# Every second low part of the gate tiles on GpSimd, one-hots with a PSUM operand, and picks on eight places for the low ranks

## The chip, the cores and the metric

One of the cores of a Trainium2 chip runs the whole kernel. The metric is the device time of one execution in microseconds, lower is better; it is given as the median of several executions.

## The reference, cut to what matters

Two layers work on 512 tokens of width 1024. Each layer has a token mixer (not touched here) and then a feed-forward part that picks experts by product keys. Only that part matters for the change:

```
q = (ht @ w_q).reshape(t, 8, 2, 128)
sc = einsum('thid,hikd->thik', q, keys)            # 16 score rows of 128 keys per token
top_s, top_i = lax.top_k(sc, 16)
cand = top_s[:, :, 0, :, None] + top_s[:, :, 1, None, :]
best_s, best_pos = lax.top_k(cand.reshape(t, 8, 256), 16)
i1 = take_along_axis(top_i[:, :, 0], best_pos // 16)
i2 = take_along_axis(top_i[:, :, 1], best_pos % 16)
gates = softmax(best_s)                            # experts = i1 * 128 + i2
act = einsum('thkd,td->thk', u_tab[experts], hb)   # u_tab, v_tab: 16384 rows of 1024
out = einsum('thk,thkd->td', gates * gelu(act), v_tab[experts])
```

## The kernel before, in words

**The stream of tiles.** All weights of a layer, and both expert tables as dense matrices, come as one stream of 298 tiles of 128 x 1024 float32: 18 for the input projection, 8 for the output, 16 for the queries, 128 tiles of `u_tab` (from index `U0`) and 128 of `v_tab` (from `EV0`). SyncE loads a tile into one of three buffers `w_raw`. ScalarE copies it rounded to fp32r (`hi`, line 755, `w_hi`), and somebody subtracts (`lo`, `w_lo = w_raw - w_hi`): VectorE on line 1593 or GpSimd on line 696. TensorE multiplies in three passes, high by high, high by low and low by high, 24 matmuls for a tile (`project`, line 1037). There are two buffers of `w_hi` and of `w_lo`, so both parts of tile n+2 can only be made once TensorE has finished tile n (semaphore `s_tile`), and tile n+2 waits for both (`s_wh`, `s_wl`). A buffer of `w_raw` is given back to SyncE when both are made.

**Two kinds of tokens.** Of the 512 tokens, 352 (`TD`) go through the dense product with all 16384 experts. The other 160 have their own expert rows gathered from HBM by indirect DMAs: 160 gathers of `u` rows and 160 of `v` rows per layer, 128 rows of 4 KB each. The gathers go through a ring of five buffers (`RING`). GpSimd issues them in order (line 708); gather k+5 waits until VectorE has used gather k (`s_gd`). VectorE uses a `u` gather with one multiply-and-sum on line 2087.

**The stages of the 128 u tiles of a layer.** Call n the index of a u tile.

- Routing, n up to about 41: beside the tiles, VectorE finds the candidates, the best 16 pairs and the indices of each of four blocks of 128 tokens. `picked(tt, a)` (lines 2175 to 2185) turns the place of each pair (128 places, `HK`: 8 heads times 16 ranks) into a key by three operations on a 128 x 2048 tile `pick`: compare, multiply, sum. It runs twice per block. In this stage GpSimd makes the low parts of tiles 2 to 38 (`POOL_LO0` to `POOL_LO1`) and issues 16 early gathers. When VectorE has finished with the routing, it waits for GpSimd's last low part and goes on with the gate stage.
- Gates, n from 42 to 101 (`GATE0`, `GATE1`): tokens are handled four at a time, a "quad". There are 88 quads; `quads_of(n)` gives one to even n and two to odd n. For each quad VectorE makes the one-hot matrices of both key indices (`one_hots`, line 2109, 128 x 1024 elements: `iota` compared with `idxT`, both in SBUF), ScalarE scales one half by the gate (line 960, four operations a quad), TensorE multiplies them (four matmuls, lines 1521 and 1535), and ScalarE copies the result out of PSUM (line 991). Four buffers `oneh`, two PSUM banks. Part of the gate matrices stays in SBUF, and part is stored to HBM in bursts of four.
- The rest, n from 102, then 128 tiles of `v_tab` (line 1553), beside them the `v` gathers on VectorE (line 2099).

**Orders written out by hand.** There is no scheduler; each engine runs its own program in order. In step n VectorE does `U_GATHERS[n]` gathers (1 or 2, seven in four tiles of the gate stage), the one-hots of quads of n+1, and `lo` of tile n+2. ScalarE does the scaling of quads of n, `hi` of n+2, the gelu of tile n (line 967), and the copies of the quads of n. GpSimd has a list `POOL_GATE_LO` of gate tiles whose low parts it would make; it is empty, so in the gate stage GpSimd only issues gathers. The code for it stands in GpSimd's loop over n from `GATHER0` to `GATE1`:

```
used += U_GATHERS[n]
if n + 2 in POOL_GATE_LO:
    pool.wait_ge(s_wl, l * STREAM + U0 + n + 2)
    lo(l, U0 + n + 2)
while k < used + RING:
    gather(l, k)
    k += 1
```

Its counterpart on VectorE skips `lo` for a tile of that list, and before the `lo` of the tile behind one waits for it on `s_wl`.

Of the kernel before, what the change touches and what calls it, by code (L numbers as in the profile page):

```python
# [9 lines left out]
ALU = mybir.AluOpType  # L10
ACT = mybir.ActivationFunctionType
AX = mybir.AxisListType

P = 128
# [44 lines left out]
PH = 8  # L59
TOPK = 16  # L60
HK = PH * TOPK
# [34 lines left out]
GATE0 = 42  # L96
GATE1 = 102
GATE_LOOP = 8
OH_SLOTS = 4
# [6 lines left out]
def quads_of(n):  # L106

    if not GATE0 <= n < GATE1:
        return []
    i = n - GATE0  # L110
    first = i // 2 * 3 + i % 2
    return [q for q in ([first] if i % 2 == 0 else [first, first + 1]) if q < QUADS]
# [28 lines left out]
    U_GATHERS[_n] = 2 if _n % 5 in (1, 3) else 1  # L141
U_GATHERS[GATE1 + 4] = U_GATHERS[GATE1 + 14] = 1
assert sum(U_GATHERS) + EARLY == UG and U_GATHERS[N_KEYS - 1] == 0, sum(U_GATHERS)
POOL_GATE_LO = []
V_GATHERS = [0] + [2 if _b % 4 == 3 or _b in (33, 65, 97) else 1 for _b in range(1, N_KEYS - 1)] + [0]
assert sum(V_GATHERS) == UG, sum(V_GATHERS)

# [33 lines left out]
class Steps:  # L181
# [16 lines left out]
    def link(self, ins):  # L198

        ins.then_inc(self.sem, 1)  # L200
        self.n += 1
        self.eng.wait_ge(self.sem, self.n)


def build(nc, xT, cT, final_g, adaw, wst, params, keysT, u_0, u_1, v_0, v_1, g_dram, a_dram, outT):
    u_rows, v_rows = (u_0, u_1), (v_0, v_1)
    ctx = ExitStack()
    with ctx:
        def sb(name, shape, dt=F32, where=ctx):
            return where.enter_context(nc.sbuf_tensor(name, shape, dt))  # L210
# [10 lines left out]
        iota = sb("iota", [P, P])  # L221
# [51 lines left out]
        def pcol(name, n=None):  # L273
            a, w = PCOL[name]
            return par[:, a:a + w]
# [110 lines left out]
        route = sb("route", [P, 3, HK], where=r2)  # L386
# [4 lines left out]
        oneh = [sb(f"oneh{s}", [P, 2, QUAD, P], where=r3) for s in range(2)]  # L391
# [261 lines left out]
        def _(pool):  # L653
# [59 lines left out]
            for l in range(LAYERS):  # L713
# [16 lines left out]
                for n in range(GATHER0, GATE1):  # L730
# [3 lines that stand above are left out]
# [845 lines left out]
        def _(dve):  # L1579
            steps = Steps(dve, s_dve, s_dset)  # L1580
            link = steps.link
            v = nc.vector
# [43 lines left out]
            for j, p0, w in ((0, 0, 2), (0, 64, 4), (1, 0, 8), (1, 64, 16)):  # L1626
                ins = v.tensor_scalar(inv_count[p0:p0 + 64, j, :], inv_count[p0:p0 + 64, j, :], float(w), None, ALU.min)
# [18 lines left out]
            for l in range(LAYERS):  # L1646
# [22 lines left out]
                for k in range(KT):  # L1669
                    ins = v.tensor_scalar(h32[:, k, :], h32[:, k, :], mod[:, 0, k:k + 1], None, ALU.add)  # L1670
                ins.then_inc(s_h32, 1)

                q = lambda n: tiny[:, n, :]
# [143 lines left out]
                def averaged(p0, j, src):  # L1817

                    r = slice(p0, p0 + 64)
                    v.tensor_tensor(pooled[r, j, 0:PAD], src[r, j, PAD:2 * PAD], inv_count[r, j, :], ALU.mult)  # L1820
                    return v.tensor_scalar(pooled[r, j, PAD:], src[r, j, 2 * PAD:], inv_count[r, j, PAD - 1:PAD], None, ALU.mult)

                for n in range(N_IN):
# [21 lines left out]
                    if n == 13:  # L1845
                        dve.wait_ge(s_pm, l + 1)
                        for j in range(2):
                            ins = v.tensor_scalar(mixed[:, 4 + j, :], bank[2 + 4 * j][:, :], pcol("pool_scale")[:, j:j + 1], None, ALU.mult)
# [25 lines left out]
                    if n == 11:  # L1874
                        link(v.tensor_tensor(pool_a[:, 1, 15:], pool_c[:, 1, 15:], pool_c[:, 1, 7:PJW - 8], ALU.add))
                        for p0, j, src in ((0, 1, pool_c), (64, 1, pool_a)):
                            ins = averaged(p0, j, src)
# [225 lines left out]
                def one_hots(q):  # L2103

                    n = l * QUADS + q
                    if n >= OH_SLOTS:
                        dve.wait_ge(s_gm, n - OH_SLOTS + 1)
                    full = [P, 2, QUAD, P]
                    v.tensor_tensor(oneh[q % OH_SLOTS][:, :, :, :], iota[:, :].unsqueeze(1).unsqueeze(1).broadcast_to(full),  # L2109
                                    idxT[:, 0:2, q * QUAD:(q + 1) * QUAD].unsqueeze(3).broadcast_to(full),  # L2110
                                    ALU.is_equal).then_inc(s_oh, 1)

                first_at = bank[5][:, 0:HK]
# [5 lines left out]
                full = [P, PH, TOPK, TOPK]  # L2119
                each = lambda f: [f(h) for h in range(PH)][-1]  # L2120
                pk = pick[:, :, :]
                pk4 = pk.rearrange("p (h k) j -> p h k j", h=PH)
# [52 lines left out]
                def picked(tt, a):  # L2175

                    at, of, op, rows = ((first_at, pair_start[:, :], ALU.is_ge, step_at),
                                        (col_at, iota[:, 0:TOPK], ALU.is_equal, row_at))[a]
                    link(v.tensor_tensor(pk, at.unsqueeze(2).broadcast_to([P, HK, TOPK]),
                                         of.unsqueeze(1).broadcast_to([P, HK, TOPK]), op))  # L2180
                    link(v.tensor_tensor(pk4, pk4, rows.unsqueeze(2).broadcast_to(full), ALU.mult))
                    if a == 0 and tt >= 2:

                        dve.wait_ge(s_rtt, l * (NT - 1) + tt - 1)
                    link(v.reduce_sum(route[:, a, :], pk, AX.X))

                def gated(tt):

# [31 lines left out]
                for tt in range(NT):  # L2220
                    first_rows(tt)
                    candidates(tt)
                    best_pairs()
                    shifted()
                    decoded()
                    early = EARLY_GATHERS[tt]
                    if tt == 1:
                        dve.wait_ge(s_htr, l + 1)
                    for a in range(2):
                        for _ in range(early // 3):  # L2230
                            gather_u(gathered)
                            gathered += 1
                        picked(tt, a)
                    for _ in range(early - 2 * (early // 3)):
                        gather_u(gathered)
                        gathered += 1
                    gated(tt)
                    if tt == 2:
                        extra_gathers()

                def coefs(b):

                    g, j = b // GROUP, b % GROUP
                    s = g % 2
                    if j == 0:

                        dve.wait_ge(s_gin[s], (l * (GROUPS // 2) + g // 2 + 1) * 16)
                        dve.wait_ge(s_ain[s], (l * (GROUPS // 2) + g // 2 + 1) * 16)
                    act = act_in[s][:, j // 2, j % 2, :]
                    v.tensor_tensor(coef[:, b % 2, 0:GSPILL].rearrange("p (c t) -> p c t", c=GSTORED),  # L2250
                                    act[:, 0:GSPILL].rearrange("p (c t) -> p c t", c=GSTORED),
                                    gates[s][:, :, j, :], ALU.mult)
                    v.tensor_tensor(coef[:, b % 2, GSPILL:TD].rearrange("p (c t) -> p c t", c=GKEPT),  # L2253
                                    act[:, GSPILL:TD].rearrange("p (c t) -> p c t", c=GKEPT),
                                    stages[:, :, b, :], ALU.mult).then_inc(s_cp, 1)
# [6 lines left out]

                k = EARLY
                assert gathered == EARLY
                dve.wait_ge(s_htv, 2 * l + 2)
                dve.wait_ge(s_wl, l * STREAM + POOL_LO1)
                for n in range(GATHER0, N_KEYS):
                    for _ in range(U_GATHERS[n]):
                        gather_u(k)
                        k += 1  # L2270
                    if n == GATE0 - 1:
                        dve.wait_ge(s_idx, l * (NT - 1) + NT - 1)
                    for q in quads_of(n + 1):
                        one_hots(q)
                    if n == N_KEYS - 2:
                        dve.wait_ge(s_gv, (l + 1) * QUADS + 2)
                    if n >= N_KEYS - 2:
                        coefs(n - (N_KEYS - 2))
                    if n + 2 not in POOL_GATE_LO:
                        if n + 1 in POOL_GATE_LO:  # L2280
                            dve.wait_ge(s_wl, l * STREAM + U0 + n + 2)
                        lo(l, U0 + n + 2)
                    if n >= N_KEYS - 2:
                        coef_low(n - (N_KEYS - 2))
                assert k == UG

                k = 0
# [106 lines left out]
```

## Time and profile before

| | us |
|---|---|
| median of 3 runs | 2919.84 |
| lowest and highest | 2913.98, 2921.28 |
| the profiled execution, its own time | 2915.25 |
| its span | 2913.5 |
| TensorE busy in the span | 2854.0 (98%) |
| VectorE busy | 2495.6 (86%) |
| ScalarE busy | 1447.4 (50%) |
| GpSimd busy | 998.9 (34%) |

The span is cut into stretches by what the engines work on. The u tiles of the first layer start near 400 us, its gate stage runs from about 571 to 876 us, and its v tiles start at 980 us. For the second layer the gate stage runs from about 1987 to 2293 us. A matmul's recorded duration overlaps the next one's, so TensorE's progress is read from the starts of its pieces in the chain of waits, not from durations of single matmuls.

### The profile page before, as it was taken

Reading aid. Unit: us, or ns where it says so; the run is one execution under the profiler, and the core shown is the slowest. Engines: PE = TensorE matmul, PEld = TensorE weight load, DVE = VectorE, ACT = ScalarE, POOL = GpSimd, SP = SyncE. Lnnn points to the kernel's source line nnn. Section 1 sums busy time; section 2 is a strip of 40 time slices with the busy share of each in tenths; the row PEclk is TensorE's granted clock in tenths of the full one; section 3 lists DMA queues with packets and bytes.
Section 4 is the critical chain, followed back from the end, with each engine's and each line's share of the span. In section 5 each row is a group of like instructions: output and inputs, shape, how many; then the busy total and the mean of one; then the engine's idle time right before and its main releaser. Section 6 shows DMA issues by size and latency. Waiting matters only on the chain.

```text
span 2913.5 us, 48879 instructions
## 1 busy us (share of the span) xinstructions
PE 2854.0 (98%) x17734; PEld 2666.3 (92%) x17734; DVE 2495.6 (86%) x4773; ACT 1447.4 (50%) x2309; POOL 998.9 (34%) x773
## 2 busy tenths in 40 slices
PE   6999999999999999999999999999999999999998
PEld 4777789999999999999978778999999999999998
DVE  5667789799996899999986779988999879999998
ACT  3345234488883433333353532447888634333333
POOL 1000027644443443444400000675444333443442
PEclk9999999999999999999999999999999999999999
DMA  7435647899999999999931122679999999999996
GB/s 277 169 114 187 255 145 239 304 363 380 393 330 383 360 381 381 382 386 385 379 117 66 66 69 84 200 245 348 394 375 372 345 379 364 387 380 377 378 386 250
DMA packets 261579, 857.75 MB, mean 294 GB/s; under 512 B 25664, under 2 KB 58688, under 8 KB 254784
## 3 DMA queue, kind: packets, MB, share of 16 engines
q1 hardware_dynamic: 158336, 445.11, 41.8%
q0 software_dynamic: 98496, 381.73, 34.9%
q10 hardware_dynamic: 4608, 29.36, 2.4%
q8 instruction: 51, 0.84, 0.1%
q14 instruction: 88, 0.72, 0.1%
HBM read 778.50 MB, written 77.59 MB: 294 GB/s over the span
## 4 chain that ended last, share of the span: by engine, by line
PE 83%; DMA 7%; DVE 5%; ACT 3%; issue 2%; SPq 0%; POOL 0%; DVEq 0%; ACTq 0%
PE banks L1037 39%; PE banks L1553 29%; PE banks L1521 4%; DMA w_raw<-wst 4%; PE banks L1358 2%; DMA ring<-u,gidx 2%; PE banks L1053 2%; DVE w_lo L1593 2%; PE banks L1102 1%; ACT w_hi L755 1%; PE banks L1441 1%; DMA pj<-adaw 1%; DVE ring L2087 1%; DVE oneh L2109 1%; PE banks L1199 0%
## 5 line engine op out<-in xcount | busy, mean ns | idle before, releaser
L755 ACT ACTIVATE w_hi<-w_raw 128x1024 fp32r<-128x1024 f32 x596 | 630.3, 1058 | 747.8 <-PE banks L1037 575.0
L1037 PE MATMUL banks<-hH,w_hi 128*128 128x352 f32 (+1 forms) x2528 | 866.4, 343 | 4.8 <-issue 1.7
L1593 DVE TENSOR_TENSOR w_lo<-w_raw,w_hi 128x1024 fp32r<-128x1024 f32 x522 | 638.4, 1223 | 269.8 <-ACT w_hi L755 247.8
L1037 PE MATMUL banks<-hH,w_lo 128*128 128x352 f32 (+1 forms) x2528 | 845.4, 334 | 0.0
L1037 PE MATMUL banks<-hL,w_hi 128*128 128x352 f32 (+1 forms) x2528 | 845.0, 334 | 0.0
L708 POOL DMA_INDIRECT ring<-v,gidx x320 | 396.1, 1238 | 593.0 <-DVE vacc L2099 534.6
L708 POOL DMA_INDIRECT ring<-u,gidx x320 | 399.1, 1247 | 464.7 <-DVE gact L2087 438.9
L1037 PEld LDWEIGHTS banks<-hH,w_hi 128*128 128x128 f32 x2528 | 474.8, 188 | 53.5 <-issue 24.4
L1553 PE MATMUL banks<-c_lo_late,w_hi 128*128 128x352 f32 x1536 | 494.0, 322 | 0.0
L1037 PEld LDWEIGHTS banks<-hH,w_lo 128*128 128x128 f32 x2528 | 474.3, 188 | 19.5
L1037 PEld LDWEIGHTS banks<-hL,w_hi 128*128 128x128 f32 x2528 | 475.1, 188 | 17.4 <-issue 0.5
L2099 DVE SCALAR_TENSOR_TENSOR vacc<-ring,gcoef,vacc 128x1024 f32<-128x1024 f32 x316 | 404.2, 1279 | 7.4 <-DVE vacc L2099 0.5
L2087 DVE CUSTOM_DVE_ANT_0 ring<-ring,banks 128x1024 f32<-128x1024 f32 x256 | 304.1, 1214 | 50.4 <-DMA ring<-u,gidx 26.3
L696 POOL TENSOR_TENSOR w_lo<-w_raw,w_hi 128x1024 fp32r<-128x1024 f32 x74 | 177.8, 2402 | 472.1 <-ACT w_hi L755 471.2
L1553 PE MATMUL banks<-c_hi_late,w_hi 128*128 128x352 f32 x1024 | 334.5, 327 | 1.7 <-DVE w_lo L1593 1.5
L1553 PE MATMUL banks<-c_hi_first,w_hi 128*128 128x352 f32 x1024 | 332.7, 325 | 0.0
L1553 PE MATMUL banks<-c_hi_first,w_lo 128*128 128x352 f32 x1024 | 330.8, 323 | 0.0
L1553 PE MATMUL banks<-c_hi_late,w_lo 128*128 128x352 f32 x1024 | 329.9, 322 | 0.0
L1553 PEld LDWEIGHTS banks<-c_lo_late,w_hi 128*128 128x128 f32 x1536 | 289.2, 188 | 0.0
L960 ACT ACTIVATE oneh<-oneh,idxT 128x128 f32<-128x128 f32 x704 | 215.3, 395 | 8.6 <-DVE oneh L2109 6.9
L2109 DVE TENSOR_TENSOR oneh<-iota,idxT 128x1024 f32<-128x1024 f32 x176 | 209.7, 1218 | 0.0
L1012 ACT ACTIVATE c_hi_late<-coef 128x352 fp32r<-128x352 f32 x128 | 63.8, 498 | 289.3 <-DVE coef L2253 289.3
(345 smaller groups left out, 3986.4 us busy)
## 6 DMA issues: line engine op xcount, KB each, us to landing
w_raw<-wst SPq DMA_DIRECT2D x596, 512.0 KB
activations<-act_out SPq DMA_DIRECT2D x128, 352.0 KB
act_in<-activations SPq DMA_DIRECT2D x64, 704.0 KB
gate_matrices<-stages ACTq DMA_DIRECT2D x32, 896.0 KB
gates<-gate_matrices SPq DMA_DIRECT2D x64, 448.0 KB
ada_buf<-adaw POOLq DMA_DIRECT2D x24, 1024.0 KB, 6.5
nrm<-adaw POOLq DMA_DIRECT2D x8, 1024.0 KB, 5.1
pj<-adaw POOLq DMA_DIRECT2D x7, 1024.0 KB, 7.2
```

What stands on the lines that cost most here:

```text
L696: pool.tensor_tensor(w_lo[g % 2][:, :, :].rearrange("p a b -> p (a b)"), w_raw[:, g % RAWS, :], w_hi[g % 2][:, :, :].rearrange("p a b -> p ...
L708: pool.indirect_dma_start(out=ring[:, n % RING, :], out_offset=None, in_=rows[:, :], in_offset=bass.IndirectOffsetOnAxis(ap=gidx[:, k % UG ...
L755: nc.scalar.activation(w_hi[g % 2][:, :, :].rearrange("p a b -> p (a b)"), w_raw[:, g % RAWS, :], ACT.Copy).then_inc(s_wh, 1)
L960: ins = nc.scalar.activation(oh, oh, ACT.Copy, scale=idxT[:, 2, q * QUAD + t:q * QUAD + t + 1])
L1012: nc.scalar.activation(c_hi[(b + 2) % GROUP], coef[:, b % 2, :], ACT.Copy).then_inc(s_chi, 1)
L1037: last = mm(bank[s][:, 0:t.stop - t.start], a[s][:, k, :], b[:, k, t], start=(k == 0 and a is w_hi and b is hH), stop=(k == KT - 1 and a i ...
L1521: last = mm(bank[2 + u % 2][:, t * P:(t + 1) * P], oneh[u % OH_SLOTS][:, 0, t, :], oneh[u % OH_SLOTS][:, 1, t, :], start=True, stop=True)
L1553: last = mm(bank[k][:, TG:T], w[j % 2][:, k, :], c[j], start=(first and w is w_hi and c is c_hi), stop=(final and w is w_lo))
L1593: v.tensor_tensor(w_lo[g % 2][:, :, :].rearrange("p a b -> p (a b)"), w_raw[:, g % RAWS, :], w_hi[g % 2][:, :, :].rearrange("p a b -> p (a ...
L2087: v.tensor_tensor_reduce(ring[:, n % RING, :], ring[:, n % RING, :], rhs, 1.0, 0.0, ALU.mult, ALU.add, gact[:, k:k + 1]).then_inc(s_gd, 1)
L2099: ins = v.scalar_tensor_tensor(acc[:, :], ring[:, n % RING, :], gcoef[:, k:k + 1], acc[:, :], ALU.mult, ALU.add)
L2109: v.tensor_tensor(oneh[q % OH_SLOTS][:, :, :, :], iota[:, :].unsqueeze(1).unsqueeze(1).broadcast_to(full), idxT[:, 0:2, q * QUAD:(q + 1) * ...
```

## The change

- `POOL_GATE_LO` is filled with the 29 gate tiles n that stand behind a tile of two quads: 44, 46, ... 100. GpSimd makes their low parts, VectorE no longer does.
- The one-hots read the column numbers from PSUM (`first_at`, in bank 5) instead of SBUF (`iota`). One copy a layer puts them there, behind the routing.
- `picked` works on two boxes. The low ranks (0 to 7 of each head) are compared with 8 places only, the others with 16: 8 x 8 x 8 = 512 and 8 x 8 x 16 = 1024 elements instead of 2048. So each of the three operations is now two.

```diff
-POOL_GATE_LO = []
+POOL_GATE_LO = [n for n in range(GATE0, GATE1) if len(quads_of(n - 1)) == 2]
...
-                    v.tensor_tensor(oneh[q % OH_SLOTS][:, :, :, :], iota[:, :].unsqueeze(1).unsqueeze(1).broadcast_to(full),
+                    v.tensor_tensor(oneh[q % OH_SLOTS][:, :, :, :], first_at.unsqueeze(1).unsqueeze(1).broadcast_to(full),
                                     idxT[:, 0:2, q * QUAD:(q + 1) * QUAD].unsqueeze(3).broadcast_to(full),
                                     ALU.is_equal).then_inc(s_oh, 1)
...
-                    link(v.tensor_tensor(pk, at.unsqueeze(2).broadcast_to([P, HK, TOPK]),
-                                         of.unsqueeze(1).broadcast_to([P, HK, TOPK]), op))
-                    link(v.tensor_tensor(pk4, pk4, rows.unsqueeze(2).broadcast_to(full), ALU.mult))
+                    boxes = [(slice(0, 8), 8), (slice(8, TOPK), TOPK)]
+                    by_rank = lambda t: t.rearrange("p (h k) -> p h k", h=PH)
+                    for ranks, w in boxes:
+                        box = [P, PH, 8, w]
+                        ins = v.tensor_tensor(pk4[:, :, ranks, 0:w], by_rank(at)[:, :, ranks].unsqueeze(3).broadcast_to(box),
+                                              of[:, 0:w].unsqueeze(1).unsqueeze(1).broadcast_to(box), op)
+                    link(ins)
+                    for ranks, w in boxes:
+                        ins = v.tensor_tensor(pk4[:, :, ranks, 0:w], pk4[:, :, ranks, 0:w],
+                                              rows[:, :, 0:w].unsqueeze(2).broadcast_to([P, PH, 8, w]), ALU.mult)
+                    link(ins)
...
-                    link(v.reduce_sum(route[:, a, :], pk, AX.X))
+                    for ranks, w in boxes:
+                        ins = v.reduce_sum(by_rank(route[:, a, :])[:, :, ranks], pk4[:, :, ranks, 0:w], AX.X)
+                    link(ins)
...
+                link(v.tensor_copy(first_at, iota[:, :]))
                 dve.wait_ge(s_htv, 2 * l + 2)
                 dve.wait_ge(s_wl, l * STREAM + POOL_LO1)
```

## Rows read from the trace of the kernel before

**Rows 1.** The chain of waits, gate stages of both layers: start us, duration us, what.

```profile
579.59 1.78 PE banks L1521 x16
...
591.66 3.81 PE banks L1037 x24
595.47 0.89 PE banks L1521 x8
...
871.62 3.81 PE banks L1037 x24
...
2008.23 3.81 PE banks L1037 x24
...
2288.28 3.81 PE banks L1037 x24
```

**Rows 2.** Engine busy time by stretch, first layer: routing (two), gates (three).

```profile
core 0: us, PE busy (x) PEld busy (x) DVE busy (x) ACT busy (x) POOL busy (x), PEclk, DMA share, GB/s
400.00:490.00 90.00, 90.00 (x560) 86.93 (x559) 86.53 (x356) 37.10 (x51) 58.32 (x30) 1.00 0.63 205
490.00:572.00 82.00, 80.69 (x500) 78.24 (x500) 64.13 (x141) 36.28 (x52) 56.61 (x33) 1.00 0.80 270
572.00:660.00 88.00, 88.00 (x617) 88.00 (x616) 86.08 (x106) 77.27 (x161) 41.14 (x31) 1.00 0.97 371
660.00:750.00 90.00, 89.39 (x622) 88.83 (x622) 82.06 (x102) 79.47 (x165) 38.45 (x30) 1.00 1.00 388
750.00:880.00 130.00, 129.91 (x905) 129.48 (x904) 122.87 (x153) 111.26 (x234) 56.81 (x46) 1.00 0.95 349
```

**Rows 3.** VectorE's waits, both routing stages: total us, times, longest us.

```profile
DVE ring L2087 <- POOL w_lo L696: 11.5, 1, 11.5
DVE ring L2087 <- POOL w_lo L696: 12.0, 1, 12.0
```

**Rows 4.** Groups of VectorE instructions by line and shape: busy us, mean ns.

```profile
L1593 DVE TENSOR_TENSOR w_lo<-w_raw,w_hi 128x1024 fp32r<-128x1024 f32 x522 | 638.4, 1223 | 269.8 <-ACT w_hi L755 247.8 <-issue 20.2
L2109 DVE TENSOR_TENSOR oneh<-iota,idxT 128x1024 f32<-128x1024 f32 x176 | 209.7, 1218 | 0.0
L2181 DVE TENSOR_TENSOR pick<-pick,banks 128x2048 f32<-128x2048 f32 x16 | 36.6, 2287 | 0.6
L2185 DVE TENSOR_REDUCE route<-pick 128x128 f32<-128x2048 f32 x16 | 36.6, 2286 | 0.6
L1779 DVE TENSOR_TENSOR smat<-seg,cbm 128x512 f32<-128x512 f32 x16 | 10.3, 684 | 0.0
```

**Rows 5.** Single lines 696 (GpSimd) and 2212 (VectorE): duration ns min/median/max.

```profile
L696 POOL TENSOR_TENSOR w_lo<-w_raw,w_hi x74: 2372/2402/2428, 403.7 to 1967.6; 128x1024 fp32r<-128x1024 f32 x74
L2212 DVE COPY ggate<-pick x2: 1406/1836/2266, 507.9 to 1922.8; 128x32 f32<-128x32 f32 x2
```

**Rows 6.** Timeline of GpSimd in the gate stage: start us, duration us, instruction, idle before.

```profile
822.29 0.94 POOL L708 DMA_INDIRECT ring<-u,gidx  x1 [1.73 <-DVE gact L2087]
823.69 1.43 POOL L708 DMA_INDIRECT ring<-u,gidx  x1 [0.45 <-DVE gact L2087]
828.22 0.94 POOL L708 DMA_INDIRECT ring<-u,gidx  x1 [3.10 <-DVE gact L2087]
```

**Rows 7.** Timeline of VectorE, the same stretch.

```profile
820.80 1.21 DVE L2087 CUSTOM_DVE_ANT_0 ring<-ring,banks 128x1024 f32<-128x1024 f32 x1
...
823.09 2.35 DVE L2109 TENSOR_TENSOR oneh<-iota,idxT 128x1024 f32<-128x1024 f32 x2
825.36 1.22 DVE L1593 TENSOR_TENSOR w_lo<-w_raw,w_hi 128x1024 fp32r<-128x1024 f32 x1
826.50 1.21 DVE L2087 CUSTOM_DVE_ANT_0 ring<-ring,banks 128x1024 f32<-128x1024 f32 x1
```

**Rows 8.** Timeline of ScalarE, the same stretch.

```profile
824.09 1.06 ACT L755 ACTIVATE w_hi<-w_raw 128x1024 fp32r<-128x1024 f32 x1 [1.21 <-issue]
```

**Rows 9.** VectorE's waits for gathers in the first layer's gate stage.

```profile
DVE ring L2087 <- DMA ring<-u,gidx: 8.5, 6, 2.2
```

**Rows 10.** The chain of waits, around 741 us.

```profile
724.79 16.54 DMA ring<-u,gidx
...
742.58 2.28 DVE oneh L2109 x2
744.86 0.27 issue
745.13 1.13 PE banks L1521 x8
```

## The prediction

> **What bounds the kernel now.** I read the chain of waits first, because a change that takes work off VectorE and puts it on GpSimd only matters where one of them ends the chain. In the gate stage the chain is TensorE alone, and it runs like a clock [rows 1]: a u tile takes 3.81 us, one quad behind it 0.89, two quads 1.78. So two tiles with their three quads take 2 x 3.81 + 3 x 0.89 = 10.29 us. From tile 46 (591.66) to tile 100 (871.62) there are 27 such pairs: 277.8 us if TensorE never waits, and 279.96 were taken. In the second layer it is 2288.28 - 2008.23 = 280.05. So TensorE loses 2.1 and 2.2 us, 4.4 us in both gate stages together. That is all that relief of VectorE can bring there.
>
> The busy time by stretch agrees, and adds what the chain doesn't say [rows 2]: in the gate stage VectorE is busy 86.08 of 88 us, ScalarE 77.27, and the DMA engines 95 to 100%. Four resources are nearly full, TensorE is the fullest, and the others have to hit its beat. Where VectorE is late, it is so because a gather has not landed: six waits, 8.5 us in the first layer's gate stage [rows 9]. One of them stands in the chain [rows 10]: a gather issued at 724.79 landed 16.54 us later, the two one-hots came late, and their quads started late on TensorE. So the thing to watch is the ring of gathers, which hangs on GpSimd.
>
> In the routing stage VectorE, when done, waits 11.5 and 12.0 us for GpSimd's last low part [rows 3]. Its routing work is not late for anything.
>
> **The change, part by part.**
>
> *Picks.* A compare, multiply or sum over 2048 elements takes 2.29 us; 512 take 0.68, 1024 take 1.22 [rows 4]. Two boxes: 0.68 + 1.22 = 1.90, so 0.38 saved each. There are 3 x 2 x 4 x 2 = 48 of them: 18.4 us off VectorE, 9.2 a layer. The time goes into the wait for GpSimd at the end of routing, which grows from 11.5 to about 21 us [rows 3]. TensorE is busy 90.00 of 90 us beside the bulk of it [rows 2], so nothing comes nearer. I count 0; the end below is -1 us a layer if some early gather is used sooner, above 0.
>
> *The copy to PSUM.* Two copies of 128 x 128, under 0.68 us each by the 512-element row [rows 4], inside the same wait: 0.
>
> *One-hots from PSUM.* The form with two SBUF operands takes 1.218 us, multiplications with one PSUM operand lie on the same line (2.287 for twice the size) [rows 4]. So the duration stays: 0. What it may change is GpSimd: its gather issues take 0.94 us, but 1.43 when one begins beside a running one-hot (823.69 against 823.09) [rows 6, 7]. That half microsecond I take back for about half of the issues; it goes into the ring's account below. The Trainium skill, "SBUF — State Buffer", section "SBUF: two separate sides", has it that VectorE and GpSimd share one pair of ports under an exclusive lock, taken by VectorE operations with two SBUF inputs. By that rule the one-hots would no longer hold up GpSimd's subtraction at all, and the trace agrees as far as it goes: the stretched issue above, and a copy of 32 elements that took 1.4 and 2.3 us in the routing stage, where GpSimd subtracts [rows 5].
>
> *Low parts on GpSimd.* 29 tiles x 2 layers. VectorE gives up 58 x 1.223 = 70.9 us [rows 4], GpSimd takes on 58 x 2.402 = 139.3 us [rows 5]. Is the low part itself in time? `hi` starts at 824.09, when the even tile n has ended, and VectorE's `lo` follows at 825.36 [rows 7, 8]. On GpSimd it would end near 825.3 + 2.4 = 827.7. Tile n+2 needs it after a quad, a tile and two quads: 824.03 + 0.89 + 3.81 + 1.78 = 830.5. Slack 2.8 us: 0 for the low part itself.
>
> The price is behind it in GpSimd's queue. The gathers released in step n now stand behind `lo` of n+2. The slots that VectorE freed around 822 and 823 were given to new gathers at 822.29 and 823.69 [rows 6]; now the first goes out at 827.8 and the second 1.25 later: 5.4 us later each. Those of the odd step, freed near 827.6 and so far issued from 828.22 [rows 6], wait for these two: about 1 to 2 us later. With three to four gathers in a pair of tiles, about half of them of each kind, a slot loses 3 us on average. A slot comes round every 5/7 of four tiles, 20.58 x 5/7 = 14.7 us. So far issue to use leaves some 13 us for the gather; now 10, for the worst ones 8. Gathers under the bursts of gate stores take more than that: the one at 724.79 took 16.5 [rows 10].
>
> Against it stands VectorE's relief: 1.14 us a pair of tiles (a low part, starts lie 1.14 apart [rows 7]), so it arrives earlier at the next gather, and the wait of the `lo` behind GpSimd's is for `hi` anyway. Also fewer transfers lie in the DMA queues when issues come late, so each lands sooner after its issue. I put it so: the gate stage has three places a layer where a late gather reaches TensorE (they make up the 2.1 us). A slot 3.0 us later, less two pairs' relief of 1.1 each, leaves about 1 us more at each place: 3 x 2 x 1 = +6 us. This is an estimate from the rows above; the ends are -4.4 us (all of TensorE's waits go) and +18 us (each place passes on the 3.0 us in full).
>
> *Sum.* 2915.25 us (the profiled execution; 2913.5 of it span, 1.75 around it) + 0 + 0 + 0 + 6 = 2921.3 us. The median of the runs shown is 4.6 us above that execution, which gives 2925.8. The next median may lie on either base; I take 2924.
>
> **The rivals.**
>
> *A. VectorE's relief removes the late gathers.* If the ring's slots have enough room in spite of GpSimd, the one-hots come early and TensorE's 4.4 us go: 2919.84 - 4.4 = 2915.4. For it: VectorE is 98% busy in the first stretch of gates. Against: its waits there are for gathers, which it can't shorten [rows 9].
>
> *B. Nothing moves.* The picks' time goes into a wait, the relief into idle time, the ring holds: 2920. For it: 98% TensorE.
>
> *C. The ring becomes the bound, slower.* GpSimd's queue holds back the gathers of even steps by 5.4 us; under the bursts of gate stores a gather takes 12 to 16 us, a slot cycle then takes longer than 14.7 us, VectorE is late in several pairs in a row, its one-hots are late, and TensorE waits. It decides from the point at which issue to landing exceeds 10 us for more than three gathers in a row. Price: 3 us at each of six places, +18 us: 2938. For it: DMA share 1.00 at 388 GB/s in the middle stretch [rows 2], the row of 16.54 us. Against: gathers outside the bursts cause no wait at all.
>
> *D. The two engines stop each other.* If VectorE's operations wait out a GpSimd subtraction after all (with the gathers' multiply, say), each of the 58 puts up to 2.4 us on VectorE against 1.14 taken off: 58 x 1.26 = +73 us, 2993. Against it: in the routing stage GpSimd's subtractions took 2372 to 2428 ns [rows 5] beside a VectorE that was busy 86.53 of 90 us [rows 2]. The copy of 32 elements shows that such stops exist, but for a form that the gate stage doesn't have.
>
> **How the numbers follow.** Forecast (a small loss, +1 to +9 us): 0.42. B, with A's smaller part (-4 to +1): 0.24. A: 0.07. C: 0.23. D: 0.04. A measurement of this kernel can tell about 0.3% from no change, 8.8 us; the runs shown lie 7.3 us apart. Faster by more than that: 0.08, since the chain has only 4.4 us to give and the rest would be another base. Slower by more: most of C, D and the edge of the forecast, 0.32. Same: 0.60. Range: from 2911 (A on the lower runs) to 2939 (C).
>
> **What would show it.** In the changed profile: GpSimd has 132 subtractions instead of 74, near 2.40 us each; if they are longer, D. VectorE's busy time falls by about 89 us. Its wait at the end of routing grows to about 21 us; if it doesn't, the picks are mispriced. One-hots stay at 1.22 us. Gather issues in the gate stage are near 0.94 us each. From tile 46 to tile 100: 283 us rather than 280 by the forecast, 278 by A, 286 or more by C. VectorE's waits for gathers in a gate stage grow from 8.5 us to over 20; if they stay below 10, the account of the ring is wrong, and with it the forecast. Most wrong would be a gain of more than 10 us: then TensorE's beat in the gate or routing stage was not what the chain shows.

## The result and the profile after

The changed kernel takes 2944.26 us, median of 4 runs (2937.6 to 2949.99), against 2918.28 us for the kernel before beside it (4 runs). The ratio is 1.009, 95% interval 1.0074 to 1.0105: it is 26 us slower. The forecast was 2924 us, the range ended at 2939. The profiled execution's span went from 2913.5 to 2940.9 us, +27.4. Two executions, one of the kernel before and one of the version with both mends, took 4019 and 4714 us at a granted clock of 0.65 and 0.56 where all others have 0.99; no median or ratio below includes them.

The page's head shows what the change did, and that it did what it says: VectorE gave up 80.6 us of busy time, GpSimd took on 88.3.

```profile
span 2940.9 us, 48931 instructions
...
PE 2865.1 (97%) x17734; PEld 2673.7 (91%) x17734; DVE 2415.0 (82%) x4765; ACT 1448.8 (49%) x2309; POOL 1087.2 (37%) x831
...
L696 POOL TENSOR_TENSOR w_lo<-w_raw,w_hi 128x1024 fp32r<-128x1024 f32 x132 | 317.3, 2404 | 665.2 <-ACT w_hi L755 665.2
...
L2109 DVE TENSOR_TENSOR oneh<-banks,idxT 128x1024 f32<-128x1024 f32 x176 | 209.7, 1219 | 0.0
```

GpSimd's 132 subtractions take 2.404 us each, the one-hots 1.219 us: neither became longer than before. The time is between the operations. (A few small operations of the routing stage did become longer; they are named below.) This is the chain of waits of the changed kernel, first layer (start, duration, what); it answers to [rows 1].

```profile
575.63 3.81 PE banks L1037 x24
...
591.51 3.81 PE banks L1037 x24
...
884.48 3.81 PE banks L1037 x24
888.28 0.89 PE banks L1535 x8
889.17 7.61 PE banks L1037 x48
```

From tile 46 (591.51) to tile 100 (884.48) it is now 293.0 us, where it was 280.0, and in the second layer 293.7 against 280.1. From tile 43 to tile 101 the two stages grew from 300.5 and 300.8 to 313.5 and 314.6 us: 26.8 of the 27.4 us of span are here. TensorE's beat itself is the same, 3.81 and 0.89 us. It loses at three places a layer: at tiles 56 to 58 (5.3 and 5.8 us in the two layers), 75 and 76 (3.1 and 2.6) and 84 to 86 (5.9 and 5.6). Each lies just behind one of the layer's four bursts of gate stores; the second burst costs 0.7 and 1.8 us. The kernel before loses 1.1 and 1.3 us at tile 76, 0.7 and 0.2 at tile 86, and nothing at tiles 56 to 58. The first place in the chain of the changed kernel:

```profile
622.37 3.82 PE banks L1037 x24
...
626.27 1.07 ACT w_hi L755
...
627.50 2.41 POOL w_lo L696
629.91 0.14 issue
630.05 0.95 POOL ring L708
631.00 0.30 issue
631.30 15.13 DMA ring<-u,gidx
...
647.69 1.15 DVE oneh L2109
648.84 1.40 issue
650.24 1.33 PE banks L1521 x8
```

Read it as one sentence: tile 52 ends, ScalarE rounds tile 54, GpSimd subtracts, issues one gather, then the next, this one takes 15.13 us, VectorE uses it and makes a one-hot, and only then TensorE has its quad. GpSimd's timeline there (start, duration, instruction, idle before) shows three issues in a heap behind the subtraction:

```profile
627.50 2.41 POOL L696 TENSOR_TENSOR w_lo<-w_raw,w_hi 128x1024 fp32r<-128x1024 f32 x1 [2.35 <-ACT w_hi L755]
630.05 0.95 POOL L708 DMA_INDIRECT ring<-u,gidx  x1
631.30 0.94 POOL L708 DMA_INDIRECT ring<-u,gidx  x1 [0.30 <-issue]
632.55 1.65 POOL L708 DMA_INDIRECT ring<-u,gidx  x1 [0.31 <-issue]
637.79 2.42 POOL L696 TENSOR_TENSOR w_lo<-w_raw,w_hi 128x1024 fp32r<-128x1024 f32 x1 [3.59 <-ACT w_hi L755]
```

The same gather in the kernel before, where tile 52 starts at the same time (622.52 us), first its issue, then its use on VectorE:

```profile
630.22 0.94 POOL L708 DMA_INDIRECT ring<-u,gidx  x1 [3.91 <-DVE gact L2087]
...
640.25 1.22 DVE L2087 CUSTOM_DVE_ANT_0 ring<-ring,banks 128x1024 f32<-128x1024 f32 x1
```

It left only 1.1 us sooner, but had landed within 10.0 us. So in the changed kernel it left late, and it also took 5 us longer. The gather two before it fared the same. It no longer leaves ahead of the burst, whose first store goes out at 623.2 us: issued at 624.2 us it took 13.7 us, and 6.7 us in the run with the list empty (below), where it left at 621.7. The six gathers that stand in the chain at the six places all belong to odd steps. Each came second or fourth in such a heap, 3.7 or 4.6 us after its slot was free.

And VectorE's waits in the first layer's gate stage (total us, times, longest) answer to [rows 9], where there were 8.5 us in six waits, the longest 2.2:

```profile
DVE w_lo L1593 <- ACT w_hi L755: 32.7, 23, 2.8
DVE ring L2087 <- DMA ring<-u,gidx: 32.3, 18, 3.4
```

### The profile page after: what moved, and what is told of

Same layout as the page of the kernel before. It is cut to its first block, busy times and chain, and to the rows that moved or that the text cites. A ratio compares the mean times of both kernels' runs of the same rounds, so it can differ in the third digit from the quotient of the medians.

```text
span 2940.9 us, 48931 instructions
## 1 busy us (share of the span) xinstructions
PE 2865.1 (97%) x17734; PEld 2673.7 (91%) x17734; DVE 2415.0 (82%) x4765; ACT 1448.8 (49%) x2309; POOL 1087.2 (37%) x831
## 4 chain that ended last, share of the span: by engine, by line
PE 77%; DMA 10%; DVE 6%; ACT 3%; issue 2%; POOL 1%; SPq 0%; DVEq 0%; ACTq 0%; POOLq 0%
PE banks L1037 38%; PE banks L1553 25%; DMA w_raw<-wst 6%; PE banks L1521 4%; DMA ring<-u,gidx 3%; PE banks L1358 2%; PE banks L1053 2%; DVE w_lo L1593 2%; ACT w_hi L755 2%; PE banks L1102 1%; PE banks L1441 1%; DMA pj<-adaw 1%; DVE vacc L2099 1%; DVE oneh L2109 1%; DVE ring L2087 1%
## 5 line engine op out<-in xcount | busy, mean ns | idle before, releaser
L1593 DVE TENSOR_TENSOR w_lo<-w_raw,w_hi 128x1024 fp32r<-128x1024 f32 x464 | 567.9, 1224 | 313.7 <-ACT w_hi L755 311.5
L696 POOL TENSOR_TENSOR w_lo<-w_raw,w_hi 128x1024 fp32r<-128x1024 f32 x132 | 317.3, 2404 | 665.2 <-ACT w_hi L755 665.2
L708 POOL DMA_INDIRECT ring<-u,gidx x320 | 348.7, 1090 | 208.2 <-DVE gact L2087 150.1
L2109 DVE TENSOR_TENSOR oneh<-banks,idxT 128x1024 f32<-128x1024 f32 x176 | 209.7, 1219 | 0.0
```

The source lines that it names most:

```text
L696: pool.tensor_tensor(w_lo[g % 2][:, :, :].rearrange("p a b -> p (a b)"), w_raw[:, g % RAWS, :], w_hi[g % 2][:, :, :].rearrange("p a b -> p ...
L708: pool.indirect_dma_start(out=ring[:, n % RING, :], out_offset=None, in_=rows[:, :], in_offset=bass.IndirectOffsetOnAxis(ap=gidx[:, k % UG ...
L1593: v.tensor_tensor(w_lo[g % 2][:, :, :].rearrange("p a b -> p (a b)"), w_raw[:, g % RAWS, :], w_hi[g % 2][:, :, :].rearrange("p a b -> p (a ...
L2109: v.tensor_tensor(oneh[q % OH_SLOTS][:, :, :, :], first_at.unsqueeze(1).unsqueeze(1).broadcast_to(full), idxT[:, 0:2, q * QUAD:(q + 1) * Q ...
```

## The experiments

Theory Q: gathers queue behind GpSimd's low part, a ring slot loses its room, and under the gate stores VectorE's one-hots come late. Rivals: N, the one-hots or picks themselves cost the time; S, the two engines block each other at SBUF. The kernel before was run again beside each group of runs, so it has several medians; each ratio is to the one beside it. The medians are of 2 to 11 runs, those of the kernel before of up to 28. The column "gate stages" is from tile 46 to tile 100 in each layer, read from the starts on TensorE; its beat alone needs 277.8.

| kernel | median us | ratio to before (95%) | gate stages us |
|---|---|---|---|
| before | 2918.3 to 2920.2 | | 280.0, 280.1 |
| changed | 2944.3 | 1.009 (1.0074 to 1.0105) | 293.0, 293.7 |
| changed, list empty | 2918.3 | 0.9995 (0.9985 to 1.0005) | 280.1, 280.3 |
| before, list alone | 2957.0 | 1.0142 (1.0116 to 1.0168) | 297.0, 298.2 |
| changed, gathers first | 2914.3 | 0.9986 (0.9975 to 0.9998) | 278.2, 277.9 |
| before, ring of 4 | 2944.7 | 1.0092 (1.0072 to 1.0112) | 289.8, 293.6 |
| changed, stores in 8 parts | 2914.8 | 0.9982 (0.9972 to 0.9992) | 278.1, 278.1 |
| before, stores in 8 parts | 2913.8 | 0.9978 (0.9966 to 0.9989) | 278.1, 277.9 |
| changed, 15 tiles of 29 | 2941.9 | 1.0063 (1.0045 to 1.0081) | 289.7, 289.6 |
| gathers first, one-hots from SBUF | 2918.5 | 0.9992 (0.9981 to 1.0003) | 281.8, 278.9 |
| gathers first, stores in 8 parts | 2915.6 | 0.9985 (0.9975 to 0.9995) | 277.9, 277.9 |
| before, picks alone | 2918.4 | 1.0001 (0.999 to 1.0012) | 279.9, 280.3 |
| before, wait alone | 2923.5 | 1.0015 (1.0004 to 1.0026) | 281.1, 283.3 |

**Without the low parts.**

```diff
-POOL_GATE_LO = [n for n in range(GATE0, GATE1) if len(quads_of(n - 1)) == 2]
+POOL_GATE_LO = []
```

> The changed kernel with the list of tiles on GpSimd empty again: one-hots from PSUM and the shorter picks stay. Theory Q (gathers queue behind GpSimd's low part, a ring slot loses 3 us and more, and under the gate stores VectorE's one-hots come late): the gate stages from tile 46 to tile 100 fall back to about 280 us each (changed kernel about 293), total 2916 to 2920. Rival N (the new one-hots or picks cost the time): stays near 2944. Theory S (GpSimd and VectorE block each other at the SBUF ports): as Q here.

2918.3 us: N falls. One-hots from PSUM and the picks together change nothing that can be measured in the time; the 26 us hang on the list. GpSimd's gather issues in the gate stage did become shorter, 0.95 us on average where the kernel before has 1.29.

**The low parts alone**, on the kernel before.

```diff
-POOL_GATE_LO = []
+POOL_GATE_LO = [n for n in range(GATE0, GATE1) if len(quads_of(n - 1)) == 2]
```

> The kernel before with nothing but the 29 low parts a layer on GpSimd; one-hots keep both operands in SBUF, picks stay long. Q: the same delay of the gathers, so 2940 to 2948, with one-hots at 1.22 us. S: one-hots with two SBUF operands meet GpSimd's subtraction of 2.4 us in each pair of tiles, some of them take up to 3.6 us, and the total is beyond 2955. N: 2918.

2957.0 us, 13 more than the changed kernel and more than Q alone expected. Here S is real. Groups of the first gate stage (busy us, mean ns, idle before), then a single line's minimum, median and maximum:

```profile
L2109 DVE TENSOR_TENSOR oneh<-iota,idxT 128x1024 f32<-128x1024 f32 x88 | 126.7, 1466 | 0.0
L708 POOL DMA_INDIRECT ring<-u,gidx x107 | 140.4, 1312 | 41.4 <-DVE gact L2087 22.3 <-issue 16.6
L696 POOL TENSOR_TENSOR w_lo<-w_raw,w_hi 128x1024 fp32r<-128x1024 f32 x29 | 77.6, 2676 | 71.5 <-ACT w_hi L755 71.4
```

```profile
L2109 DVE TENSOR_TENSOR oneh<-iota,idxT x176: 1207/1218/3435, 572.8 to 2328.4; 128x1024 f32<-128x1024 f32 x176
```

A one-hot took up to 3.4 us, the mean 1.47; the subtractions 2.68 instead of 2.40. The issues of gathers take 1.31 us, hardly more than the 1.29 of the kernel before; the changed kernel has 1.09. So the operand in PSUM is worth 13 us beside GpSimd's subtraction and this queue. The Trainium skill, "SBUF — State Buffer", section "SBUF: two separate sides", has it that of a VectorE operation with two SBUF inputs and a GpSimd operation that reads SBUF, the second to start waits until the first has ended; the trace agrees, by the 3.4 us above. It is not what makes the changed kernel slow, for there the one-hots take 1.219 us.

**Gathers ahead of the low part.**

```diff
-                    if n + 2 in POOL_GATE_LO:
-                        pool.wait_ge(s_wl, l * STREAM + U0 + n + 2)
-                        lo(l, U0 + n + 2)
                     while k < used + RING:
                         gather(l, k)
                         k += 1
+                    if n + 2 in POOL_GATE_LO:
+                        pool.wait_ge(s_wl, l * STREAM + U0 + n + 2)
+                        lo(l, U0 + n + 2)
```

> The changed kernel, but in GpSimd's program the gathers of step n stand ahead of the low part of tile n+2. Q: gathers of even steps go out within 1.5 us of their slot again; those of odd steps still lose 1 to 2 us behind the low part. Most of the loss goes: 46 to 100 near 281 us, VectorE's waits for gathers from 32 to about 12 us a gate stage, total 2918 to 2926. S: the work on both engines is the same, so near 2944.

2914.3 us, below the range that was expected. The same work on every engine, 30 us less than the changed kernel, and 4 to 5 us less than the kernel before: this is what rival A of the prediction had for the change. The gate stages fall onto TensorE's beat, and VectorE's waits for gathers to 7.7 us:

```profile
DVE ring L2087 <- DMA ring<-u,gidx: 7.7, 10, 2.4
```

**A ring of four**, on the kernel before.

```diff
-RING = 5
+RING = 4
```

> The kernel before with four ring slots in use instead of five; no low part moves to GpSimd in the gate stage. A slot then comes round every 4/7 of 20.58 = 11.8 us instead of 14.7, a loss of 2.9 us, about what the change took by its queue. Q: the gate stages lose as in the changed kernel, 46 to 100 at 288 to 298 us, at the same three places under the gate stores; total 2935 to 2950. S and N: no GpSimd subtraction there and old one-hots, so 280 us and about 2919.

2944.7 us, with the old one-hots and no subtraction on GpSimd in the gate stage. A slot less is 2.9 us less room, and it costs what the change costs (here two runs only). TensorE loses at the same three places, and 1.6 and 2.6 us more behind the second burst (tile 65). So a loss of room alone, without any work moved, costs as much.

**Thinner bursts**, on the changed kernel.

```diff
-STORES = 4
+STORES = 8
```

> The changed kernel with each burst of gate stores cut into eight parts over eight tiles instead of four over four: the same bytes, half the rate. Theory Q says that a delayed gather hurts only where it also travels slowly, beside the stores. Then gathers land in 8 to 9 us there instead of over 10, and most of the 13 to 14 us that a gate stage loses goes: 46 to 100 at 282 to 286 us, total 2918 to 2930. If the loss doesn't hang on the stores, it stays near 2944.

2914.8 us, less than expected: nothing of the loss is left, though GpSimd's queue is as in the changed kernel. The gather of the chain above, issued at 631.53 us in the same heap, is now used 9.9 us later:

```profile
631.53 0.94 POOL L708 DMA_INDIRECT ring<-u,gidx  x1 [0.30 <-issue]
...
641.40 1.22 DVE L2087 CUSTOM_DVE_ANT_0 ring<-ring,banks 128x1024 f32<-128x1024 f32 x1 [1.28 <-DMA ring<-u,gidx]
```

The longest time from issue to landing in the trace is 12.5 us, and 16.5 in the changed kernel. VectorE still waits 22 times, but never long:

```profile
DVE ring L2087 <- DMA ring<-u,gidx: 19.7, 22, 1.9
```

19.7 us of waits cost nothing, while 8.5 us in six waits with one of 2.2 stand beside a loss of 2.1 us in the kernel before. So the sum of VectorE's waits doesn't tell the loss. The longest wait doesn't either: it is 2.4 us with gathers first, which loses nothing. My reading, not tried by itself: VectorE makes a late gather good in its own waits for the next rounded tile, and it has 30.6 us of these here and 42.5 with gathers first, against 8.5 in the kernel before.

**The same on the kernel before.** The edit is the same line.

> The kernel before with the same eight-part stores. Its gate stages lose 2.1 and 2.3 us at the bursts; with thinner bursts that goes, and TensorE runs on its beat: 278 us from 46 to 100, total 2 to 5 us below the kernel before. If TensorE's small losses have another cause: no difference.

2913.8 us, ratio 0.9978 (0.9966 to 0.9989). Both gate stages are on the beat. This one line brings as much as any version with the low parts moved.

**Half the tiles**, on the changed kernel.

```diff
-POOL_GATE_LO = [n for n in range(GATE0, GATE1) if len(quads_of(n - 1)) == 2]
+POOL_GATE_LO = [n for n in range(GATE0, GATE1) if n % 4 == 0]
```

> The changed kernel with only the 15 tiles 44, 48, ... 100 of a layer on GpSimd. Q: every second pair of tiles issues its gathers at once, so the mean delay of a slot is half, and VectorE has half the relief. The ring's room is crossed by less at the same bursts; loss a third to a half: total 2924 to 2934. A price per moved tile (13 of the 26 us) would give 2931; a threshold gives less than half.

2941.9 us by median; the ratio's interval (0.45 to 0.81% slower) overlaps the whole list's (0.74 to 1.05%). The gate stages lose 9.8 and 9.5 us against 13.0 and 13.6. So 15 tiles cost some 70% of what 29 do: not a price per tile, and the expectation of a third to a half was too low. But the 15 tiles are not half of the queue's delay either. Their low parts stand in steps with two gathers (`U_GATHERS[n]` is 2 for n % 4 == 2), those of the other 14 in steps with one. Read from the trace, they bring about 64% of the delay that the whole list brings (table below). This run can't tell a price by the mean delay from one by the worst.

**One-hots from SBUF with the queue set right.**

```diff
-... first_at.unsqueeze(1).unsqueeze(1).broadcast_to(full),
+... iota[:, :].unsqueeze(1).unsqueeze(1).broadcast_to(full),
```

> The version with gathers ahead of the low part (2914), but one-hots read iota from SBUF again. This prices the two-SBUF-operand form beside GpSimd alone, with the queue set right. In the run with that form some one-hots took up to 3.4 us, the mean in the gate stage was 1.47 instead of 1.22 us, some of GpSimd's subtractions 3.4 instead of 2.4. VectorE has some 35 us a gate stage free from the low parts and gives back about 22: if that stays beside TensorE's work, 2914 to 2918; if the late ones reach the one-hots that TensorE needs next, 1 us for each pair of tiles at worst, up to 2940. I expect 2916 to 2925.

2918.5 us against 2914.3; the intervals of the two ratios overlap, so the times alone don't separate them. In the traces the gate stages are 3.6 and 1.0 us longer, and single one-hots take up to 2.5 us. So the price of blocking is at most some 5 us here and was 13 with the queue wrong. That it uses up the same room is my reading.

**Both mends.** Gathers first and `STORES = 8`.

> Both mends together: gathers ahead of the low part, and gate stores in eight parts, on top of the change. Each alone brought the gate stages to 298.5 to 299.1 us from first to last quad, where TensorE's beat alone needs 298.4. So theory Q expects nothing more from both: 2911 to 2916, the same as either. If the thinner bursts also help the tiles behind the gate stage, up to 3 us less.

2915.6 us: no more than either, since there is nothing left to take; VectorE's waits for gathers are 0.2 us in the first gate stage.

**Picks alone.** The changed kernel's `picked` on the kernel before.

> The kernel before with the shorter picks alone. 9.2 us a layer less work on VectorE in a stage where TensorE is on its beat and VectorE waits for GpSimd at the end: no difference, ratio 0.999 to 1.001, and longer waits of VectorE there.

Ratio 1.0001 (0.999 to 1.0012). VectorE's wait at the end of routing grows from 11.5 us [rows 3] to 15.7, not to 21: its waits for early gathers in that stage grow too, from 5.9 to 8.8 us. Another 2 us go into small operations with two SBUF operands that now meet a GpSimd subtraction: the gate multiplications of line 2203 (line 2193 before) take 1.04 us on average where they took 0.31.

**The wait without the subtraction**, on the kernel before.

```diff
+                    if n % 2 == 0 and GATE0 <= n < GATE1 - 2:
+                        pool.wait_ge(s_wh, l * STREAM + U0 + n + 3)
                     while k < used + RING:
                         gather(l, k)
```

> The kernel before, with no low part moved, but in each even step of the gate stage GpSimd waits for the rounding of tile n+2 before it issues the gathers of step n. That is the first half of what the change puts before them: the wait of some 3 us, not the subtraction of 2.4. Q: gathers of even steps go out 3 us later instead of 5.4, those of odd steps hardly later; VectorE has no relief here. A slot loses 1.3 us on average: gate stages lose more than before at the bursts, 302 to 308 us instead of 300.5, total 2922 to 2933. If only the subtraction's work or its use of SBUF mattered: 2919.

2923.5 us, ratio 1.0015 (1.0004 to 1.0026). GpSimd computes nothing more, it only stands still ahead of the gathers, and the gate stages lose 1.1 and 3.3 us more than before, behind the same bursts. The stage's issues of gathers with what GpSimd waited for (this kernel is a line shorter, so ScalarE's line is 754):

```profile
L708 POOL DMA_INDIRECT ring<-u,gidx x108 | 142.5, 1320 | 172.7 <-ACT w_hi L754 109.3 <-DVE gact L2086 56.7 <-issue 6.6
```

109.3 us of waiting for ScalarE went in where it had waited for VectorE. The gathers of even steps leave 2.2 us later for it, those of odd steps 0.1. That is a third of the changed kernel's delay, and it costs a sixth of its loss (4.4 of 26.6 us). The rest must come with the 2.4 us of subtraction and the heap behind it.

## Why the prediction was wrong

**Right.** TensorE's beat, and that the stages had only 4.4 us to give: four versions reached 277.9 to 278.2 us, none went below. The picks, the PSUM copy and the low part's own timing at nothing. The durations of the one-hots, the subtractions and the picks (18.5 us less in all, forecast 18.4). That the ring is the thing to watch, and how much later the gathers leave. Rival C named the mechanism, its place and its sign.

How late they leave can be read for each gather: from the end of the use that frees its slot to its issue. Means over the 98 gathers of the steps 44 to 99, first layer (the second agrees within 0.2 us):

| kernel | even steps us | odd steps us | all us | gate stage us |
|---|---|---|---|---|
| before | 0.3 | 0.4 | 0.4 | 280.0 |
| changed, gathers first | 0.3 | 1.7 | 1.1 | 278.2 |
| before, wait alone | 2.6 | 0.6 | 1.5 | 281.1 |
| changed, 15 tiles of 29 | 3.7 | 1.7 | 2.6 | 289.7 |
| changed | 5.1 | 2.8 | 3.8 | 293.0 |
| changed, stores in 8 parts | 5.6 | 3.3 | 4.3 | 278.1 |

The forecast's mean of 3.0 us more was right: it is 3.4.

**The step that failed** is the price of a late slot: "A slot 3.0 us later, less two pairs' relief of 1.1 each, leaves about 1 us more at each place: 3 x 2 x 1 = +6 us." The two stages grew by 26.8 us; 25 of it is at the six places, 4.2 us each. Three things in it were wrong.

- *The landing.* The prediction had each late gather land sooner after its issue. Where it counts, the opposite happened: the gather of the chain above left 1.1 us later than in the kernel before and took 15.1 us, not 10 or less. It takes both for that, the heap and the full burst of stores. With gathers first, or with the same heap and thinner bursts, it took under 10, and the whole loss was gone. The upper end, 3.0 us passed on in full at each place, left this out.
- *The relief.* 2.2 of the 3.0 us were set off against VectorE's free time. At these bursts it saved nothing that can be seen: the run with four slots has no relief and 2.9 us less room, and costs the same as the changed kernel. It isn't worth nothing everywhere. With gathers first the gathers still leave 0.7 us later than in the kernel before, and yet TensorE is on its beat.
- *The places.* The kernel before has two places a layer where a late gather reaches TensorE (tiles 76 and 86), not three. The count of three came true by luck: the place at tiles 56 to 58, which costs 5.3 and 5.8 us, cost nothing before.

The chance of C, 0.23, was too low for the same reason. Its condition, more than three gathers in a row over 10 us from issue to landing, is met in the run with the list empty, where the gathers leave as in the kernel before: there are six in a row behind the first burst and eight behind the third. The trace of the kernel before has no landing times, only [rows 10].

**Smaller misses.** "In the gate stage the chain is TensorE alone" is too strong: in the first layer it leaves TensorE at 667.5 us and comes back with the last lines of [rows 10], at 745.1. The times from tile 46 to tile 100 stand all the same. VectorE's busy time fell by 80.6 us, not 89: low parts and picks gave what was forecast, but some 4 us went into small operations of the routing stage that met a GpSimd subtraction, as in the run with the picks alone; the rest is spread thinly. For that reason, and by longer waits for early gathers, its wait at the end of routing is 15.6 us and not 21. The copy of [rows 5] reads one operand, so it was no case of an operation with two SBUF inputs; those small operations are. Gather issues in the gate stage take 1.09 us, not 0.94.

**Left open.** How the loss grows with the delay. With the wait alone, 15 tiles and the whole list the gathers leave 1.1, 2.2 and 3.4 us later than before, and the first gate stage loses 1.1, 9.8 and 13.0 us; but VectorE's relief differs too among the three. How much of a place's 4.2 us is lateness and how much is slower landing was read from single gathers only.

## What to carry to other kernels

An engine that also issues transfers has a queue: work put ahead of an issue delays it by the work and by whatever the work waits for, here 3 us for a rounded tile and 2.4 of subtraction. Before moving work there, count the room of the ring (slots times the time between uses, less issue to landing) at its worst stretch, not at its mean, and put the issues first. A transfer that leaves late may also travel in a worse stretch and take longer. The order of two statements was worth 30 us, the choice of engine at most some 4.

## What the runs showed of the hardware

A VectorE operation with both operands in SBUF and a GpSimd subtraction do stop each other: one-hots of 1.22 us took up to 3.4, subtractions of 2.40 up to 3.37. With one operand in PSUM, neither was ever longer than 1.223 and 2.430 us in the changed kernel. The stop can end with the subtraction: in the changed kernel's routing stage a VectorE multiplication of 128 x 128 elements, both operands in SBUF, took 2.10 us beside one, where the kernel before has 0.31 on average.

```profile
470.21 2.39 POOL L696 TENSOR_TENSOR w_lo<-w_raw,w_hi 128x1024 fp32r<-128x1024 f32 x1 [1.81 <-ACT w_hi L755]
...
470.64 2.10 DVE L2203 TENSOR_TENSOR route<-bestv,gsum 128x128 f32<-128x128 f32 x1
```

GpSimd's issue of an indirect DMA is stretched too. In the kernel before's first gate stage the 58 issues that begin beside a one-hot with two SBUF operands take 1.58 us on average, the 50 others 0.94; with the one-hots' operand in PSUM and no low parts moved, those beside a one-hot take 0.94 too.

Halving the rate of the stores to HBM shortened the longest gather, from issue to landing, from 16.5 us to 12.5; the stage's 14.7 MB of stores went out all the same.
